# A decoder block's expert layer: 64 tokens fetched two slots at a time, against 128 tokens fetched one slot at a time

## The reference

```python
xn = rms_norm(h); p = xn @ w_in                        # combined projection
y_m = mLSTM branch (4 heads); y_r = RWKV-7 branch (16 heads)
h = h + (sig(g_m) * (y_m @ P_m) + sig(g_r) * (y_r @ P_r)) @ w_out
h = h + peer_ffn(rms_norm(h)); out = rms_norm(h)

# peer_ffn, per token and head (8 heads): 16384 experts, each one row of u and one of v
q  = xt @ w_query                                      # 8 heads x 2 halves x 128
s  = q . sub_keys                                      # 2 x 128 scores
v1, i1 = top_k(s[0], 16); v2, i2 = top_k(s[1], 16)
best, ci = top_k(v1[:, None] + v2[None, :], 16)        # 16 of 256 pairs
idx = e1 * 128 + e2; gate = softmax(best)
act = gelu(xt . expert_u[idx])                         # 8 x 16 = 128 experts a token
out = sum((gate * act) * expert_v[idx])
```

## Time and profile before

| | |
|---|---|
| median of three runs | 4581.39 us |
| the profiled execution's own time | 4579.21 us |
| its span, first to last instruction | 4577.5 us |
| TensorE (PE) busy | 4489.7 us, 98% |
| VectorE (DVE) busy | 2460.4 us, 54% |
| GpSimd (POOL) busy | 2176.9 us, 48% |
| ScalarE (ACT) busy | 1335.7 us, 29% |
| granted TensorE clock, mean | 0.991 |

### The profile page before, as it was taken

How to read it: one execution, slowest core, us unless ns; L and a number is a source line. 1 busy time by engine, 2 the same in 40 slices (tenths; PEclk the granted TensorE clock), 3 DMA queues, 4 the chain that set the end, 5 groups by cost and what they waited for, 6 DMA issues and landing times.

```text
span 4577.5 us, 71791 instructions
## 1 busy us (share of the span) xinstructions
PE 4489.7 (98%) x27300; PEld 3883.3 (85%) x27300; DVE 2460.4 (54%) x3876; ACT 1335.7 (29%) x1281; POOL 2176.9 (48%) x866
## 2 busy tenths in 40 slices
PE   7999999999999998999999999999999999999998
PEld 5777777778787787988989999999889999999997
DVE  4344444334554524665654787783356664656564
ACT  3323332332322212222223344442222222222223
POOL 4332332233334443444444444445577766777774
PEclk9999999999999999999999999999999999999999
DMA  3222222222224432333333444445777775777772
GB/s 121 88 89 82 89 79 88 83 86 82 106 87 147 142 124 77 120 118 116 124 113 131 158 151 177 175 151 220 268 267 259 266 259 192 258 260 262 260 261 110
DMA packets 195688, 714.70 MB, mean 156 GB/s; under 512 B 14264, under 2 KB 104632, under 8 KB 126672
## 3 DMA queue, kind: packets, MB, share of 16 engines
q1 hardware_dynamic: 143216, 495.08, 30.2%
q0 software_dynamic: 18432, 134.23, 7.7%
q10 hardware_dynamic: 33888, 83.11, 4.7%
HBM read 635.16 MB, written 77.10 MB: 156 GB/s over the span
## 4 chain that ended last, share of the span: by engine, by line
PE 84%; issue 10%; POOL 3%; DVE 2%; DMA 1%; ACT 0%; POOLq 0%; DVEq 0%; SPq 0%; ACTq 0%
PE ps L338 17%; PE ps L340 16%; PE ps L339 16%; PE ps L1903 9%; PE ps L1904 9%; PE ps L1905 9%; POOL wl L333 3%; PE ps L1607 2%; PE ps L1865 1%; PE ps L1759 0%; DVE cacc L1234 0%; PE ps L1601 0%; PE ps L1738 0%; PE ps L1737 0%; PE ps L1736 0%
## 5 line engine op out<-in xcount | busy, mean ns | idle before, releaser
L333 POOL TENSOR_TENSOR wl<-raw,wh 128x2048 fp32r<-128x2048 f32 x396 | 1841.4, 4650 | 2232.1 <-ACT wh L329 2232.0
L338 PE MATMUL ps<-xh,wh 128*128 128x448 f32 (+1 forms) x3904 | 1519.2, 389 | 30.1 <-DVE xl L1098 18.9
L340 PE MATMUL ps<-xh,wl 128*128 128x448 f32 (+1 forms) x3904 | 1485.4, 380 | 0.0
L339 PE MATMUL ps<-xl,wh 128*128 128x448 f32 (+1 forms) x3904 | 1484.9, 380 | 0.0
L329 ACT ACTIVATE wh<-raw 128x2048 fp32r<-128x2048 f32 x396 | 758.7, 1916 | 2192.0 <-PE ps L340 1217.5
L338 PEld LDWEIGHTS ps<-xh,wh 128*128 128x128 f32 x3904 | 736.6, 189 | 157.6 <-issue 36.0
L340 PEld LDWEIGHTS ps<-xh,wl 128*128 128x128 f32 x3904 | 736.2, 189 | 116.2
L339 PEld LDWEIGHTS ps<-xl,wh 128*128 128x128 f32 x3904 | 737.0, 189 | 112.4 <-issue 7.7
L1903 PE MATMUL ps<-gah,wh 128*128 128x448 f32 x2048 | 748.9, 366 | 6.7 <-POOL wl L333 5.8
L1904 PE MATMUL ps<-gal,wh 128*128 128x448 f32 x2048 | 748.7, 366 | 0.0
L1905 PE MATMUL ps<-gah,wl 128*128 128x448 f32 x2048 | 748.5, 365 | 0.0
(11 more groups left out here) (314 smaller groups left out, 3768.4 us busy)
## 6 DMA issues: line engine op xcount, KB each, us to landing
raw<-stream SPq DMA_DIRECT2D x396, 1024.0 KB
gelu_scratch<-preb ACTq DMA_DIRECT2D x128, 224.0 KB, 1.9
gates_scratch<-stage ACTq DMA_DIRECT2D x14, 2048.0 KB, 6.7
gt<-gates_scratch SPq DMA_DIRECT2D x32, 896.0 KB, 8.9
act<-gelu_scratch SPq DMA_DIRECT2D x32, 896.0 KB, 10.6
mergegate_scratch<-sgb ACTq DMA_DIRECT2D x32, 256.0 KB, 2.1
sgm<-mergegate_scratch SPq DMA_DIRECT2D x32, 256.0 KB, 2.7
h_in<-x_t SPq DMA_DIRECT2D x4, 1024.0 KB, 8.8
```

The costliest lines, as they stand in the source:

```text
L333: pool.tensor_tensor(wl[s][:, :], raw[s][:, :], wh[s][:, :].bitcast(F32), ALU.subtract).then_inc(w_lo, 1)
L338: pe.matmul(dst, w_h, h[:, kx, lo:], start=start, stop=False)
L339: pe.matmul(dst, w_h, l[:, kx, lo:], start=False, stop=False)
L340: return pe.matmul(dst, w_l, h[:, kx, lo:], start=False, stop=stop)
```

## The change

128 tokens instead of 64 are fetched for (G = 128), with one slot of 128 to a fetch: 128 fetches of u rows and 128 of v rows. The other 384 tokens (N, 448 before) meet every expert. A routing head has four score units instead of six; the rest stage has therefore 40 score units instead of 16, and the gates stage has 48 steps instead of 56. The fetches are placed by two tables: two a unit in rest units 2 to 37 (72 fetches), two a unit in the first 28 value units (the other 56 of u), then from value unit 31 on three in two units (128 of v). Row buffers are three in the rest stage and five in the value stage, the two new ones in the place of the tokens' tiles, free by then. The loops of GpSimd and VectorE over these stages are written out, and the indirect DMA takes its column of indices directly. The two DMAs that put the slots of two halves side by side (`eg2`) are gone, and so is `sel2`; the last sum over fetched tokens becomes a transpose. `ym_in` becomes one semaphore in place of three.

```diff
-SC_HEAD, SC_TAIL, SC_EGT, OH = 6, 6, 2, 8
+SC_HEAD, SC_TAIL, SC_EGT, OH = 4, 6, 2, 8
-G = 64
+G = P
 N = T - G
-SLOTS = HEADS * TOPK // 2
+SLOTS = HEADS * TOPK
...
-R_GATED = F_REST - 6
+REST_FETCHES = [range(2 * r - 4, 2 * r - 2) if 2 <= r < F_REST - 2 else range(0) for r in range(F_REST)]
+N_REST = REST_FETCHES[F_REST - 3][-1] + 1
+V_FIRST = 31
+VALUE_FETCHES = [range(min(N_REST + 2 * k, SLOTS), min(N_REST + 2 * k + 2, SLOTS)) for k in range(V_FIRST)]
+for k in range(V_FIRST, NC4 * GROUPS):
+    at = SLOTS + 3 * ((k - V_FIRST) // 2) + 2 * ((k - V_FIRST) % 2)
+    VALUE_FETCHES.append(range(min(at, 2 * SLOTS), min(at + 2 - (k - V_FIRST) % 2, 2 * SLOTS)))
+ROWS_REST, ROWS = 3, 5
+ROW_AT = [n % ROWS_REST if n < N_REST + 2 else n % ROWS for n in range(2 * SLOTS)]
+ROW_LAST = [max([m for m in range(n) if ROW_AT[m] == ROW_AT[n]], default=None) for n in range(2 * SLOTS)]
+R_GATED = F_REST - 5
...
-            def fetch(j, b, table, before=0):
-                pool.wait_ge(row_used, before + j + 1)
-                pool.sem_inc(passed, 1)
-                step(pool.tensor_copy(slot[b][:, :], idx[:, bass.ds(j, 1)]))
-                pool.sem_inc(passed, 1)
-                pool.indirect_dma_start(rowb[b][:, :], None, table, bass.IndirectOffsetOnAxis(ap=slot[b][:, :], axis=0)).then_inc(row_in[b], 16)
+            def fetch(n):
+                if ROW_LAST[n] is not None:
+                    pool.wait_ge(row_used, ROW_LAST[n] + 1)
+                pool.indirect_dma_start(rowb[ROW_AT[n]][:, :], None, u_rows if n < SLOTS else v_rows,
+                                        bass.IndirectOffsetOnAxis(ap=idx[:, n % SLOTS:n % SLOTS + 1], axis=0)).then_inc(row_in[ROW_AT[n]], 16)
...
+            for r in range(F_REST):
+                split_lo(pool, score_unit(SC_REST) + r, r % 2)
+                if r == 2:
+                    pool.wait_ge(slots_ready, 1)
+                    for s in range(2):
+                        pool.wait_ge(gates_stored[s], 16 + 8 * GB)
+                for n in REST_FETCHES[r]:
+                    fetch(n)
+                if r == R_GATED:
+                    for e in range(GE):
+                        gated(0, 0, e)
+            for k in range(NC4 * GROUPS):
+                g, c = divmod(k, NC4)
+                split_lo(pool, U_PEER + k, c % 2)
+                if k == 1:
+                    pool.wait_ge(w_used, U_PEER)
+                for n in VALUE_FETCHES[k]:
+                    fetch(n)
+                if g < GROUPS - 1:
+                    for e in (AHEAD if g else AHEAD_1)[c]:
+                        gated(g + 1, 1 - g % 2, e)
...
-            for q in range(2):
-                act.dma_start(eg2[G * q:G * q + G, :, :], EG[0:G, :, 0, SLOTS * q:SLOTS * q + SLOTS]).then_inc(eg_in, 16)
...
+            def use(n):
+                b = rowb[ROW_AT[n]][:, :]
+                dve.wait_ge(row_in[ROW_AT[n]], 16 * ROW_BEFORE[n] + 16)
+                if n < SLOTS:
+                    dve.scalar_tensor_tensor(b, b, 1.0, xg, ALU.mult, ALU.mult, accum_out=dots[:, n:n + 1]).then_inc(row_used, 1)
+                else:
+                    dve.wait_ge(row_used, n)
+                    dve.scalar_tensor_tensor(xg, b, coef[:, n - SLOTS:n - SLOTS + 1], xg, ALU.mult, ALU.add).then_inc(row_used, 1)
...
+            def dve_values(g):
                 for c in range(NC4):
+                    k = NC4 * g + c
+                    fetched = list(VALUE_FETCHES[k - 1]) if k else []
                     dve_rows(g, c, 0)
                     dve_rows(g, c, 1)
+                    for n in fetched[:1]:
+                        use(n)
                     dve_rows(g, c, 2)
+                    for n in fetched[1:]:
+                        use(n)
+                    for e in (AHEAD if g else AHEAD_1)[c]:
+                        dve_low(g + 1, 1 - g % 2, e)
                     dve_rows(g, c, 3)
```

More of the change, by code:

```diff
@@ L637, in _ @@
-            for e in range(GE):
-                gated(0, 0, e)
-            for r in range(R_GATED, F_REST):
-                if r + 2 < F_REST:
-                    rest_lo(r + 2)
-                fetch(r, r % 2, u_rows)
-            def pool_values(g, s, j=None, table=None, before=0, ahead=AHEAD):
-                for c in range(NC4):
-                    split_lo(pool, U_PEER + NC4 * g + c, c % 2)
-                    if table is not None:
-                        fetch(j + c, c % 2, table, before)
-                    for e in ahead[c]:
-                        gated(g + 1, 1 - s, e)
@@ L652, in _ @@
-            for s in range(2):
-                pool_values(s, s, F_REST + NC4 * s, u_rows, ahead=AHEAD_1 if s == 0 else AHEAD)
-            with pool.Fori(1, G_U // 2) as i:
-                step.enter(i, 1, 2 * NC4)
-                for s in range(2):
-                    pool_values(2 * i + s, s, F_REST + NC4 * (2 * i + s), u_rows)
-                step.leave(G_U // 2 - 1)
-            for s in range(2):
-                pool_values(G_U + s, s)
-            with pool.Fori(G_V // 2, G_VEND // 2) as i:
-                step.enter(i, G_V // 2, 2 * NC4)
-                for s in range(2):
-                    pool_values(2 * i + s, s, NC4 * (2 * i + s - G_V), v_rows, before=SLOTS)
-                step.leave((G_VEND - G_V) // 2)
@@ L666, in _ @@
-            for s in range(2):
-                pool_values(GROUPS - 2 + s, s, ahead=AHEAD if s == 0 else [()] * NC4)
+            for r in range(F_REST):
[9 more added lines that the diff above has]
+                        gated(0, 0, e)
@@ L1025, in _ @@
                 act_halves(0, 0, e)
-            for r in range(R_GATED + 2, F_REST):
+            for r in range(R_GATED + 1, F_REST):
                 rest(SC_REST + r, r % 2)
@@ L1486, in _ @@
-            dve_values(G_U, 0)
-            dve.wait_ge(row_used, 2 + SLOTS)
+            for r in range(F_REST):
+                for n in REST_FETCHES[r]:
+                    use(n)
+                if r == R_GATED:
+                    for e in range(GE):
+                        dve_low(0, 0, e)
+            for g in range(8):
+                dve_values(g)
+            dve.wait_ge(row_used, SLOTS)
             dve.memset(xg, 0.0)
             dve.wait_ge(gel_ready, 1)
-            step(dve.tensor_tensor(coef[:, :], gel[:, :], eg2[:, 2, :], ALU.mult))
@@ L1500, in _ @@
+            for b in range(4):
                 dve.wait_ge(sum_out, b + 1)
-                at = H[:, 8 * b:8 * b + 8, 0:G]
-                step(dve.tensor_tensor(at, bank(b).rearrange("p (k t) -> p k t", k=8), at, ALU.add))
+                at = H[:, 4 * b:4 * b + 4, 0:G]
+                step(dve.tensor_tensor(at, bank(b).rearrange("p (k t) -> p k t", k=4), at, ALU.add))
             step(dve.memset(sum3[:, :], 0.0))
```

109 lines of the change are left out of this document (29 added, 80 removed).

## The result

The changed kernel takes 4330.25 us (median of 4 runs, 4324.7 to 4332.9) beside 4581.85 us for the kernel before in the same session. The ratio is 0.9449 with a 95% interval of 0.9432 to 0.9465, a gain of 5.5%. Forecast were 4326 us and a range of 4265 to 4430.

What follows compares the result with a forecast made beforehand. TensorE, 98% busy with matmuls spaced by their columns, was taken as the bound. From 4579.2 us, columns and gates left 4231.1; added waits gave 4324, and 2.2 for the median gave 4326 us, range 4265 to 4430.

Steps and rivals of the forecast that it cites:

- Columns: Score and value matmuls: 384 columns instead of 448 shorten units to 8.45 and 8.39 us, gaining 340 us.
- the rival in which weight loads set the spacing: Score and value matmuls: weight loads limit the gain to 173 us instead of 340, about 4423 us; chance 0.03.
- Gates: Gates stage: eight fewer steps gain 7.7 us; VectorE's work fits the shorter step, 4 us added (0 to 20).
- First fetch: Rest unit 4: fetch 3 needs a used buffer and holds up GpSimd's split; 8.4 us stall plus 1.6 clock, +10.
- Routing: Routing heads: VectorE's 59.0 us chain becomes slower than TensorE's 57.9 us, but may lag; +5 us (0 to 20).
- The rival with a meeting at every place: Routing: VectorE's chain meets all six GpSimd splits of a head, 80.5 us, 158 us more, total 4480; chance 0.03.
- Rest: Rest stage: DMA demand lengthens 36 units to 8.7 us (+10), plus 8 for three buffers; +18 us.
- The 8 us for three buffers: Rest stage: a second fetch must wait until the preceding unit's first has landed and been used; +8 us.
- Start and u phase: First value units: start +12 us (6 to 30); u rows, DMA demand lengthens 28 units to 9.2 us, +22.
- The 4.4 us for fetch 75's buffer: Start of values: fetch 75 waits for buffer 0, delaying GpSimd's next split past TensorE's need by 4.4 us.
- v phase: Value units fetching v rows: stream load queued behind each group load stalls, 1 us in each of 21 groups, +21 (0 to 105).
- the marks named ahead: Signs: splits 8.39 to 8.45 us apart, one 8 us gap, rest units 8.7, u units 9.2, stream wait per v group.

Runs made afterwards that it cites:

- 16-row fetches: Changed kernel, but every fetch except the first into each of the five row buffers brings 16 rows instead of 128: 4364.3 us, ratio 0.9522.
- two-by-two table: Changed kernel's first 29 value units, full rows/16-row fetches: gal subtraction with both operands in SBUF 299.5/304.3 us, one in PSUM 286.7/257.9 us.
- one fetch in eight: Changed kernel with the last 56 u rows fetched over 31 value units in place of 28: 4307.0 us; with eight tail score units too, 4297.0 us.
- the run without it: Each group's load issued in two parts, against the 4297.0 us version (changed kernel, eight tail score units, u rows over 31 value units): 4372.4 us, ratio 0.9535.

## Why the prediction was right, point by point

- **Columns.** Right: 8.44 and 8.43 us (8.45 and 8.39 predicted, the second from a value unit read as 9.71 in place of 9.75), so the straight line between 256 and 448 columns holds at 384 within 0.5%, and the rival in which weight loads set the spacing is out. In the rest stage the loads are listed as 100% busy again, with no effect.
- **Gates.** Right: VectorE's work fitted, the 4 us for lag were not needed.
- **First fetch.** The size is right (10.4 for 10). What it is worth was not seen: without it the time is paid later in the same stage.
- **Routing, +27 for 5.** This term was mis-sized. The sum took the chain of a head as fixed at 59.0 us, with one meeting in it. It has four in the head of the earlier trace rows: the operation of 4.73 us shown there and, on VectorE in time order,

```profile
2326.73 1.67 DVE L1374 TENSOR_TENSOR EG<-ex,sm 128x64 f32 x1
...
2356.03 2.82 DVE L1357 TENSOR_TENSOR cand<-v 128x256 f32<-128x256 f32 x1
...
2365.48 2.97 DVE L1361 TENSOR_TENSOR ex<-best 128x64 f32<-128x64 f32 x1
```

  together 10.9 us beyond the shortest durations. After the change the last reductions of the heads (L1356) follow each other by 64.1, 65.8, 66.9, 65.3, 57.8, 63.0 and 59.1 us, 442 us or 29 above 7 x 59.0. Over these heads 33 operations are lengthened, 4.7 a head, and by 15.3 us a head. So there are somewhat more meetings, and each is longer (3.2 us in place of 2.7). Splits per microsecond rose by only 7%, from 8 in 82.8 us to 6 in 58.0; before, every head from the second to the seventh met the splits at the same places, now each head meets them at others. How much the closer splits do and how much the places is not separated. The rival with a meeting at every place had the right mechanism and was too dear: the excess is a fifth of what it priced, and its 80.5 us a head counted five full meetings on top of a chain that held 10.9 us of them already. The expectation that the lag would be hidden up to the end of the tail failed with it: ScalarE waited 48.6 us in five heads for the softmax input, up to 20.4.
- **Rest, +8 for 18.** The step that failed is that a full queue lengthens the unit to 8.7: at a DMA share of 1.00 it is 8.44. Of the forecast's two figures the one from bytes at 401 GB/s (8.3 us) was right, the one from summed shares (9.0) too high. The 8 us for three buffers did not come either. What remained, 7.9 us, appears when group 0's load is issued, and 7.6 of it vanish with the bytes.
- **Start and u phase, +54.5 for 34.** Mis-sized, with half the cause. The bandwidth sum was fair (the share is 0.93 to 0.96 from 3250 to 3350 us), but VectorE's sum of 8.0 us a unit had 1.1 us for everything besides the additions and the dots, with nothing for standing still. With the measured 1.64 us, four additions to `H` (0.55 each), two dots (2.28 and 0.08 each) and gal make 8.6 us, above the unit's 8.45. With the 3.41 us of the 16-row fetches they make 10.3, and a unit there takes 304.3/29 = 10.5. The two-by-two table shows that both limits bind. The 4.4 us for fetch 75's buffer were wrong: that wait lies beside a longer one for the stream.
- **v phase, +8 for 21.** The wait came as predicted, ScalarE for the stream once a group, 21 times and up to 7.3 us; the price did not. In each group an interval of about 9.3 us is followed by one of 7.5, and TensorE waits for no split between 3450 and 4210 us. The wait even lets the subtraction in ahead of the split.
- **What hit the total.** Above the columns and gates the forecast had 93 us, measured are 98 (4329.4 - 4231.1), 2 of which are columns. Too little in routing and the u phase was offset by too much in the rest and v phases; the agreement of 4326 with 4330 is partly luck. Of the marks named ahead, the undisturbed unit, the single gap and the once-a-group wait came true; the rest units of 8.7 did not.

The Trainium skill (SBUF — State Buffer, Who interferes with whom) calls the port pair of VectorE and GpSimd an exclusive lock. The traces agree: 4.23 us for 0.42 behind a split, and 0.55 us in all 53 subtractions with one operand in PSUM.

## What to carry to other kernels

When a period gets shorter, don't carry over the duration of an engine's chain that was measured at the longer one. Find what of it is standing still (here 10.9 of 59.0 us, in four operations and not in the one that catches the eye), since that part moves with the places where the engines meet. Where two resources lie at the same height, removing one shows little or nothing; test them in a two-by-two table before calling either innocent, and relieve both at once (here one fetch in eight, 19 to 24 us of the stage). A wait off the critical path may hold other work in a good order: the run without it took 75 us more.

## What the runs showed of the hardware

- The DMA engines sustain 396 to 398 GB/s at a share of 1.00 with TensorE undisturbed, with two row fetches of 1.05 MB, a load of 1.05 MB and a store per 8.44 us.
- A fetch of 128 rows of 8 KB costs 2.54 us of the 16 DMA engines' time here and 2.75 in the kernel before, so that shares read in one kernel are a rough measure for the next.
- A subtraction on VectorE can stand still behind several GpSimd operations in a row: 6.97 us for 0.55, through two gatings and a split. Whether it comes in between them goes by how early the next GpSimd operation can start: kept out in 28 of 28 cases where ScalarE's copy was ready 0.23 us or more ahead, let in in 28 of 28 others.
- An operation with a single SBUF input can stand still too: the CAST of L1337 (`if<-i`, 128 x 64) lasts 0.19 us at its shortest and 3.54 at its longest, issued at 2025.34 beside a split.
